# Convolution products of token blocks 2 to 4 woven into the first attention block, one-row softmax sums, and a bf16 copy of layer 0's output weights

## The reference, cut to what matters

```python
def _softmax_attend(q, k, v, bias=None, sink=None):
    s = jnp.einsum('bqkgd,bnkd->bkgqn', q, k).astype(jnp.float32) * ATT_SCALE
    ...
        p = jax.nn.softmax(s, axis=-1)
    return jnp.einsum('bkgqn,bnkd->bqkgd', p.astype(v.dtype), v)

def _mixer_ab(xn, cn, p, rope, need_ctx):
    q, k, v, gb, gc, u = jnp.split(xn @ p['w_in'], _split_points(IN_WIDTHS_AB), axis=-1)
    ...
    attn = _dense_latent_attention(q, k, v, kc, vc)
    conv = gb * _short_conv(gc * u, p['conv_w'])
    y = jnp.concatenate([attn, conv], axis=-1) @ p['w_out']
```

## Time and profile before

| | |
|---|---|
| median of 3 runs | 6962.02 us |
| fastest and slowest of them | 6952.61 and 7265.59 us |
| the profiled execution, its own time | 6981.62 us |
| its span, first to last instruction, slowest core (7) | 6980.1 us |
| other cores' spans | 6909.7 to 6969.9 us |
| PE, DVE, ACT busy | 93%, 55%, 34% of the span |

### The profile page before, as it was taken

One profiled execution on the slowest core, in us unless ns is written; L12 is line 12 of the kernel. 1 busy time (PEld: TensorE's weight loads), 2 busy tenths in 40 slices (PEclk: granted clock), 3 DMA queues, 4 the chain that ended last, 5 costly groups with the idle time before them and its releaser, 6 DMA issues.

```text
span 6980.1 us, 105992 instructions; the slowest of 8 cores (6909.7 to 6980.1 us)
## 1 busy us (share of the span) xinstructions
PE 6524.7 (93%) x35634; PEld 3401.5 (49%) x35634; DVE 3849.2 (55%) x6857; ACT 2389.2 (34%) x3782; POOL 225.3 (3%) x282
## 2 busy tenths in 40 slices
PE   2889999999897999999999999997989999999998
PEld 1334433433343665665675775453444444444443
DVE  1666445666666661663672663456766446374563
ACT  1666158787574110111220111555542001110111
POOL 0000000000000000000000000000000000000000
PEclk7999999999999999999999999998999999999999
DMA  9545576344747887777667868664576564866758
GB/s 184 145 125 116 109 154 125 86 107 114 180 99 162 131 135 179 111 124 184 131 113 173 138 110 211 136 122 136 206 211 115 123 137 86 201 128 150 156 106 175
DMA packets 470981, 983.07 MB, mean 141 GB/s; under 512 B 48688, under 2 KB 155952, under 8 KB 460464
## 3 DMA queue, kind: packets, MB, share of 16 engines
q0 software_dynamic: 228320, 517.78, 44.9%
q1 hardware_dynamic: 223120, 440.15, 19.8%
q10 hardware_dynamic: 19008, 18.35, 0.8%
HBM read 1275.47 MB, written 182.85 MB: 209 GB/s over the span
## 4 chain that ended last, share of the span: by engine, by line
PE 82%; DVE 5%; DMA 5%; ACT 4%; issue 3%; SPq 0%; another core or an unknown queue 0%; DVEq 0%; ACTq 0%; POOL 0%; POOLq 0%
PE pair L593 49%; PE pair L1797 32%; DMA arena<-w_mod 2%; DVE arena L1150 1%; ACT arena L1147 1%; DVE arena L1700 1%; ACT arena L683 1%; DVE arena L671 1%; PE pair L1289 1%; DMA hn<-arena 0%; DMA arena<-hn 0%; DMA q<-arena 0%; DMA arena<-w_down 0%; SPq L199 0%; DMA ud<-arena 0%
## 5 line engine op out<-in xcount | busy, mean ns | idle before, releaser
L593 PE MATMUL pair<-arena 128*128 128x512 bf16 (+6 forms) x20478 | 4111.6, 365 | 411.9 <-DMA arena<-w_mod 107.1
L593 PEld LDWEIGHTS pair<-arena 128*128 128x128 bf16 (+1 forms) x20478 | 1934.1, 101 | 2557.4 <-issue 814.5
L1797 PE MATMUL pair<-arena 128*128 128x320 bf16 (+2 forms) x14784 | 2398.8, 324 | 22.3 <-ACT arena L1810 10.0
L1797 PEld LDWEIGHTS pair<-arena 128*128 128x128 bf16 x14784 | 1441.6, 98 | 977.8 <-issue 63.2
L1700 DVE TENSOR_TENSOR arena<-arena,pair 128x320 f32<-128x320 f32 (+2 forms) x1584 | 861.0, 544 | 692.8 <-PE pair L1797 578.5
L1147 ACT ACTIVATE arena<-pair 128x1024 bf16<-128x1024 f32 (+2 forms) x896 | 867.0, 1001 | 199.7 <-PE pair L593 164.4
L1700 DVE TENSOR_TENSOR arena<-arena 128x1024 bf16<-128x1024 bf16 (+4 forms) x1224 | 789.9, 658 | 28.8 <-DMA arena<-hn 6.5
L1150 DVE TENSOR_TENSOR arena<-arena 128x1024 bf16<-128x1024 bf16 (+4 forms) x896 | 529.9, 600 | 425.1 <-ACT arena L1147 368.0
L1944 DVE SCALAR_TENSOR_TENSOR arena<-pair,arena 128x428 f32<-128x428 f32 (+3 forms) x320 | 202.0, 631 | 909.2 <-PE pair L593 873.1
L1810 ACT ACTIVATE arena<-pair 128x320 f32<-128x320 f32 (+2 forms) x264 | 125.0, 473 | 1566.0 <-PE pair L1797 1167.5
L671 DVE SCALAR_TENSOR_TENSOR arena<-arena 128x512 f32<-128x512 f32 (+6 forms) x448 | 280.3, 635 | 180.8 <-ACT arena L683 93.0
(11 more groups left out here) (69 smaller groups left out, 1884.4 us busy)
## 6 DMA issues: line engine op xcount, KB each, us to landing
arena<-w_gu POOLq DMA_DIRECT2D x88, 2048.0 KB, 17.4
arena<-w_down POOLq DMA_DIRECT2D x72, 1408.0 KB, 15.4
arena<-w_mod POOLq DMA_DIRECT2D x48, 2048.0 KB, 24.3
arena<-w_out POOLq DMA_DIRECT2D x24, 2048.0 KB, 20.5
arena<-w_in POOLq DMA_DIRECT2D x17, 2048.0 KB, 22.3
hT<-arena SPq DMA_DIRECT2D x32, 1024.0 KB, 15.6
arena<-wo POOLq DMA_DIRECT2D x16, 2048.0 KB, 10.6
arena<-x SPq DMA_DIRECT2D x56, 512.0 KB, 5.5
```

The source lines that it names most:

```text
L593: return e.matmul(out, lhsT=lhsT, rhs=rhs, start=start, stop=stop)
L1797: ins = e.matmul(out, lhsT=A[:, k, :], rhs=B[k], start=start and k == 0, stop=k == 7, skip_group_check=True)
```

## The change

1. `conv_items` keeps only blocks 0 and 1: 24 items instead of 60. The products of blocks 2, 3 and 4 (nine for each c, so 36 of 16 matmuls) are made by a new generator `conv_gen`, in steps of four matmuls in PSUM bank 7. The four `w_aux` tiles are loaded a second time for it. It is put into the side queue of query block 0 ahead of `mod_gen`, and that block's rate goes from 0.105 to 0.78. Since its input `xnA[2]` to `xnA[4]` lies where `Xb` goes, `Xb` is loaded before block 1 instead of in block 0.
2. The softmax sum of a unit is kept in one running bf16 buffer: 16 additions 128x1024, one 128x512 and one ones matmul for each unit of 17 groups, where there were 12, 5 and 5.
3. `keep` runs for both layers: eight output tiles instead of four pass the ring in the projection stage, and layer 0's 20 loads of them come from the bf16 scratch.
4. The first 9 steps of `norm2_gen(0, 3)` are added to the side queue of the last block, with its second half on DVE instead of ACT, and `xsum_gen` starts at step 24 instead of 28.

```diff
-        for t in range(4):
-            def keep(t=t):
-                u = ws.take(W[1]["wout"][t])
-                sc.dma("sp", wo_d[t], ring[u], key="wo1", reads=[s_ring[u]], writes=[sd(f"wo{t}")])
+        for k, at in enumerate((6, 13, 26, 33, 46, 53, nq + 3, nq + 11)):
+            def keep(l=k // 4, t=k % 4):
+                u = ws.take(W[l]["wout"][t])
+                sc.dma("sp", wo_d[l][t], ring[u], key="wo", reads=[s_ring[u]], writes=[sd(f"wo{l}{t}")])
                 ws.release(u)
-            items[(12, 32, 52, nq + 7)[t]]["pre"] = keep
+            items[at]["pre"] = keep
...
             gcu(0)
-            for b in range(1, 5):
-                gcu(b)
-                gb(b - 1)
-            gb(4)
+            gcu(1)
+            gb(0)
+            gb(1)
+    def conv_gen(bk):
...
+        pb = banks[bk]
+        for c in range(4):
+            u = ws.take(waux[c])
+            wt = w16(u, 384)
+            def prod(which, b, n):
+                for kq in range(4):
...
+                    sc.op("pe", f, reads=[s_ring[u], s_xnA[b]], writes=[s_bank[bk]])
+                    if kq < 3:
+                        yield 1.0
...
+            for b in (2, 3, 4):
+                n = QBLK[b][1] + (b == 4)
+                yield from prod(1, b, n)
...
+                sc.op("act", lambda e, g=g, n=n: e.activation(out=g, in_=pb[:, 0:n], func=AF.Copy),
+                      reads=[s_bank[bk]], writes=[s_g])
+                yield 1.3
+                yield from prod(2, b, n)
...
+                yield 1.3
...
+                else:
+                    yield from prod(0, b - 1, 512)
+                    conv(b - 1)
+                    yield 1.3
+            yield from prod(0, 4, 384)
+            ws.release(u)
+            conv(4)
+            yield 1.3
...
+            buf = {g: (Pb[g % 4], s_P[g % 4]) for g in gl}
+            if len(gl) < 4:
+                out += [fold(g, *buf[g], m) for g in gl]
+            else:
+                t, st = psv[0], s_psv[0]
+                for k in range(0, len(gl) - 1, 2):
+                    o, so = (t, st) if k == 0 else (psw[k // 2 % 2], s_psw[k // 2 % 2])
+                    add_at(gl[k + 1], wide(o, m), so, wide(buf[gl[k]][0], m), wide(buf[gl[k + 1]][0], m),
+                           [buf[gl[k]][1], buf[gl[k + 1]][1]])
+                    if k:
+                        add_at(gl[k + 1], wide(t, m), st, wide(t, m), wide(o, m), [st, so])
+                if len(gl) % 2:
+                    add_at(gl[-1], wide(t, m), st, wide(t, m), wide(buf[gl[-1]][0], m), [st, buf[gl[-1]][1]])
+                out.append(fold(gl[-1], t, st, m))
...
-            u = ws.take(W[0]["wout"][t]) if l == 0 else ws.take(wo_d[t], [sd(f"wo{t}")])
+            u = ws.take(wo_d[l][t], [sd(f"wo{l}{t}")])
...
-            if k >= 28:
+            if k >= 24:
                 next(xs, None)
...
-                un["rate"] = (0.105, 0.345, 0.4, 0.97, 0.4)[p]
+                un["rate"] = (0.78, 0.345, 0.4, 0.97, 0.4)[p]
...
+                if p == 4:
+                    tail[0] = norm2_gen(0, 3, 5, 0.7, "dve")
+                    side.add(itertools.islice(tail[0], 9))
             if p > 0:
-                new[0]["before"] = side.drain
+                new[0]["before"] = side.drain if p > 1 else lambda: (side.drain(), load_Xb(0, 0), load_qa(0, 1, 1))
                 new[0]["start"] = start
             units += new
+        side.add(conv_gen(7))
         for p in (2, 3, 4):
             side.add(mod_gen(0, p))
         side.weave(attn_gen(units, 2, (0, 1, 2, 3), (4, 5), 6), 1.0, 1.0)
         side.drain()
-        wout_last(side, 0, 4, 5, norm2_gen(0, 3, 5))
+        wout_last(side, 0, 4, 5, tail[0])
```

More of the change, by code:

```diff
@@ L1 @@
+import itertools
 import numpy as np
@@ L292, in build_program @@
     xn_d = dscr("xn1", [KD, 128, NT], BF16)
-    wo_d = dscr("wo1", [4, 128, 8192], BF16)
+    wo_d = [dscr(f"wo{l}", [4, 128, 8192], BF16) for l in range(2)]
     ARENA = 53208
@@ L362, in build_program @@
     assert R2.at <= p2
+    sv, (s_sv,) = Region(BASE + 28336).take("sv", 20)
+    (zb2, (s_zb2,)), (cvt2, (s_cvt2,)) = (Region(BASE + o).take(nm, w) for o, nm, w in
+                                          ((25376, "zb2", 1420), (27820, "cvt2", 512)))
+    gcB, s_gcB = Region(BASE + 26796).take("gcB", 512, 2)
+    koB, s_koB = Region(BASE + 28448).take("koB", 256, 2)
+    koB = [bf(koB[:, 256 * i:256 * (i + 1)]) for i in range(2)]
     def tset(R, spec, pre=""):
@@ L965, in conv_items @@
     def conv_items(items):
-        zseg = {4: [(0, 128, 2049), (128, 384, 2179), (384, 385, 2177)]}
         cnt = [0, 0]
@@ L972, in aproj @@
             cnt[0] += 1
-            n = QBLK[b][1] + (1 if b == 4 and which else 0)
+            n = 512
             def f():
@@ L993, in zcols @@
         def zcols(b):
-            return zseg.get(b, [(0, 512, 1 + 512 * b)])
+            return [(0, 512, 1 + 512 * b)]
         for c in range(4):
@@ L1013, in gb @@
             def gb(b, c=c):
-                f, bk, n = aproj(c, 0, b, False, b == 4)
+                f, bk, n = aproj(c, 0, b, False, b == 1)
                 p = cnt[1]
@@ L1019, in A @@
                 def A():
[L1020 to L1030 removed]
+                    m = 512 - 2 * b
@@ L1036, in gb, with taps @@
+                    sc.late("sp", aux_d[c, :, a:a + m], ko[:, 0:m], f"{sko.name}", [sko], [sd(f"aux_{b}")])
                 items.append(dict(proj=f, s1=A))
             gcu(0)
-            for b in range(1, 5):
-                gcu(b)
-                gb(b - 1)
-            gb(4)
+            gcu(1)
+            gb(0)
+            gb(1)
+    def taps(z, s_z, zc, m, c, cv, s_cv, lo=0):
+        cw = V_CONV + 3 * c
+        o = cv[:, lo:lo + m]
+        sc.op("dve", lambda e: e.tensor_scalar(out=o, in0=z[:, zc:zc + m], scalar1=vcol(cw + 1), scalar2=None,
+                                               op0=ALU.mult), reads=[s_z, s_vecs], writes=[s_cv])
+        for d, w in ((-1, 0), (1, 2)):
+            sc.op("dve", lambda e, d=d, w=w: e.scalar_tensor_tensor(
+                out=o, in0=z[:, zc + d:zc + d + m], scalar=vcol(cw + w), in1=o, op0=ALU.mult, op1=ALU.add),
+                reads=[s_z, s_vecs, s_cv], writes=[s_cv])
@@ L1520, in stage_b0 @@
         load_qa(0, 0, 1)
-        load_qa(0, 1)
-        steps = [iter(())]
+        load_qa(0, 1, 0)
+        steps, tail = [iter(())], [None]
         units = []
@@ L1533, in stage_b0 @@
                 kvs = [s_kvb[k % 2]]
-                def hook(k=k):
-                    kv_load(k + 1)
-                    if k == 1:
-                        load_Xb(0, 0)
+                hook = lambda k=k: kv_load(k + 1)
                 if b < 4:
```

72 lines of the change are left out of this document (39 added, 33 removed).

## The result

The changed kernel is slower by 1.1%: the ratio of its time to that of the kernel before is 1.0107, with a 95% interval of 1.0077 to 1.0136, so some 74 us where 42 were forecast. The median of its four runs is 7141.33 us (6977.3 us of the kernel before, with a fourth run), the fastest took 7033.8 us, and the profiled execution, 77 us above that of before, 7058.72 us.

The account below looks back on a forecast made before the run. PE, busy 93% of the span, was taken to bound the kernel. Terms -111 + 186 - 14 - 3 - 16 = +42 us on the profiled 6981.6 us gave 7024 us, a median of 7004 us; range 6940 to 7065 us.

Parts of the forecast that it names:

- The rival in which the loads are hidden: Block 0 bound by PE throughout, its last 33 groups and w_mod steps taking some 50 us: 6911 us; chance 10%.
- The rival in which bank 7 sets the pace: Block 0: each of 36 products waits 3 us for its evacuation, first part 93 us longer: 7097 us; chance 8%.
- the neutral rival: w_mod cadence 11.7 us, no wait behind bank 7, sums give their full 33 us: 6960 us, no change; chance 15%.
- part 1: Projection stage: 36 convolution items go, 116 us of PE, less one ring wait of 4 to 6 us: net -111 us.
- Part 2: Block 0 while the convolution runs, 171 of 204 groups beside it: 299 us (284 to 320).
- Part 3: Block 0 after the convolution: w_mod tiles 3 to 12 load late, 12.8 us each; block 0 lasts 442 us, +186 us.
- part 6: Pause before the feed-forward stage: early norm2 steps and `Xb` loads shorten its 19.74 us, -16 us (-20 to -5).
- Part 4: Softmax sums in blocks 1 to 4: four ones matmuls fewer a unit, -14 us (bounds -33 and +10).
- Part 5: Layer 0's output tiles in bf16: perhaps -3 us in block 4; four more casts and stores in the projection stage hidden.
- the first lands 16 us after its issue: Block 0 after the convolution: w_mod tile 3, issued at 299 us, lands 16 us later; nine more follow 12.8 us apart.
- The chain through bank 7: Block 0 beside the convolution: products wait for the copy or multiplication of the one before, 15 us (nothing to 36).
- The premise: Block 0: an exponential lasts 1.024 us, a group's four matmuls 0.87, so convolution products can fill the spare PE time.

Follow-up runs that it names:

- The first experiment: Changed kernel with the two steps of one w_mod tile after each of the twelve convolution block rounds, not all 24 behind them: ratio to the kernel before 0.9952.
- the second: Kernel before with only its w_mod steps placed late in block 0, behind 155 empty steps at rate 0.78, no convolution beside them: ratio 1.0104.
- the lighter ring: Changed kernel with w_mod steps spread, taps ahead of product gb, layer 0's output tiles fp32, layer 1's four `keep` clear of the convolution: ratio to before 0.9947.
- The best weave that was run: Changed kernel with w_mod steps spread between convolution products and the tap operations ahead of product gb: ratio to the kernel before 0.9953, die median 6877.5 us.

## Why the forecast was right in direction and mechanism, and short in size

**Direction and band.** "+42 us", within 2%, was forecast; +74 came. The range of 6940 to 7065 holds 7036, which is 6962.02 x 1.0107. The rival in which the loads are hidden fell: once three loads were in flight no two w_mod issues stood under 11.9 us apart. The rival in which bank 7 sets the pace fell too: block 0's first part was 307 us, where that rival had 392. Of the neutral rival one piece came, the sums at their full worth (-31); its two others, a cadence of 11.7 us and no wait behind bank 7, did not.

The mechanism was right and the size was short. At the start of the feed-forward stage core 7 lost 90 us where the sum has 42: part 1 missed by 23 us, parts 2 and 3 together by 26 and part 6 by 9, all too low, and parts 4 and 5 by 10 the other way. That 13 of the 90 us came back after layer 0's attention is in no term, and that the measured 74 lies as near to 42 as it does is in part luck.

**Part 3 was the deciding step, and was right.** "Tile 3 only at the end of the convolution" (issued at 1154.91, the convolution part ending at 1152), "12.8 us" (12.7 measured), PE near the forecast "under 50%" (81.41 of 160, 51%), the clock low (0.64). The 12 us after the last tile are 12 too (PE reads it at 1300.3 us, block 1 begins at 1312.2; from 1302 on the granted clock is 0.93), not the 15.7 of a slow clock throughout. The first experiment shows the place to be the cause, the second shows it enough by itself. What failed is "the first lands 16 us after its issue": some 30 us passed. I had written that `Xb` "is loaded before block 1", counted it as a move in the groups' order, and did not ask when SP's queue would be free to issue it. With `Xb` later PE had the first tile after 17.5 us, and the part is 15 us shorter. In the working this step lacked the other queue's 4.5 MB.

**Part 2 was right in its sum, and near in its parts.** 299 us against 306.7. PE's pauses were put at 17 + 15 = 32 us; 307.0 - 276.4 = 30.6 were measured. PE's work was put at 267 us and was 276.4: the 20 us that the working calls the pauses of block 1 are 8.5 us of pause in the earlier trace rows, and the rest is busy time above the price of 0.218 us a matmul. The chain through bank 7, which no row showed, was taken at 15 us; 17.2 us of waits for L1080 were measured, and with the taps moved the first part was 13 to 17 us shorter, core by core.

**Part 1 was mis-sized: -88 on core 7, -88 to -99 on the eight cores, not -111.** "One wait of 4 to 6 us" were two, 12.6 and 5.4 us, 18 together:

```profile
790.44 24.12 PE L600 MATMUL pair<-arena 128*128 128x512 bf16 x96 [12.55 <-DMA arena<-w_aux]
819.93 24.51 PE L600 MATMUL pair<-arena 128*128 128x512 bf16 x99 [5.37 <-DMA arena<-w_aux]
```

Behind each wait PE was slow too, 0.25 us a matmul instead of 0.22, which is 6 us more: the granted clock is 0.90 from 724 to 845 us, and 1.00 in the same place of the earlier trace rows. Some 4 us of the 28 that lie between 116 and 88 are left without a cause. I had counted the loads of the ring and not SP's queue, where each `keep` store stands between the small stores that DVE waits for (`DVE arena L1029 <- DMA aux<-arena`, 26.8 us). Without the extra tiles and with the rest moved, the waits for tiles go (the lighter ring).

**Part 4 was mis-sized: -14 in the text, -31 in the changed kernel and -45 in the kernel before.** Two assumptions failed. One is that "groups without side work are bound by the exponential" and win only 0.1 us a matmul: blocks 1 and 2 won 10.6 and 9.2 us, near the full 10.5 us of the matmuls. The other is that block 0 stands in no term of this part, only with its few ones matmuls in part 2; in the kernel before it wins 16 us, in the changed one nothing (466 us with either sums). There they won nothing beside the woven products and the packed loads, and those 16 us belong in the price of the weave.

**Part 5, -3 us, can't be told from nothing**, but that the four more casts are "hidden" was wrong: they take part in the waits of part 1.

**Part 6: the pause was shortened, but "-16 us" missed the other end.** The steps were moved into a block that has no time to spare for a DVE that waits: 12 us given back there, and 0 net. The forecast pause of "under 5 us" came on one core of each pair (3 us). On the other four a pause of 12.7 to 16.1 us was left, the wait ahead of the feed-forward stage's first matmuls, here on core 7:

```profile
2258.34 42.10 PE L600 MATMUL pair<-arena 128*128 128x512 bf16 x192 [0.39 <-DVE arena L1537]
2315.26 2.04 PE L600 MATMUL pair<-arena 128*128 128x512 f32 x2 [14.83 <-DVE arena L1486]
```

The 19.74 us of the earlier trace rows are 0.39 here; what is late next is the last half's additions (L1486).

**The premise.** "Block 0 has PE time to give" was weighed too little. In the earlier trace rows PE stood still for 26.4 us there and for 8.5 in block 1, which is filled. So, as an estimate, products that fill pauses could win some 18 us, in whatever order, and 13 once the sums had shortened the pauses to 21.8 (block 1 keeps 8.8 with them). The best weave that was run left 21.4 us of pause and ties with the sums alone; another order that wins was not found and is not excluded.

What stays open: why one core of each pair is behind, and where 13 of core 7's 90 us went after layer 0's attention.

## What to carry to other kernels

When work is put into an in-order queue, ask what stands behind it in every queue that it passes: here the weave's own 299 us were forecast to 3%, and the loss was loads that a ring keeps in program order, late by the whole length of the work ahead of them. Before weaving, subtract: a fair estimate of what a fill can win is the bound engine's pause minus the pause that filled stages still show (26 - 8 us here), not the length of the work. And read more than the slowest core: a pause that core 7 still shows was gone on four of the eight. Loads that must be read in one stretch are priced by their number times the cadence of the queue, and whatever other queue is free at that moment issues into the same DMA engines.

## What the runs showed of the hardware

A w_mod tile cast by POOL's queue came every 12.7 us on average in the changed kernel, and every 12.5 and 12.7 us in the one before with late loads, which has no convolution beside them. The first tile of the late row was with PE 30.6 us after its issue when SP's queue issued 4.5 MB within 6 us of it, and 17.5 us after it when SP's loads came later: transfers of the two queues took time from each other, and the load that held up PE was not let through first. In the stretch bound by loads PE was busy half of the time, and the mean granted clock fell to 0.64 on core 7 (0.69 in the two others shown), a mean between its two levels of 1.2 and 2.4 GHz; in the stretch behind it was 1.00, so that its price stays inside the stretch. The Trainium skill's page "TensorE: Matmul & The Clock Gate", part 1, tells that an engine that is little busy is throttled; the trace agrees.
